# Retention outputs and their group norm with tokens on partitions, one tile at a time, ahead of the attention projection

## The reference, cut to what matters

```python
scores = jnp.einsum('bnihd,bnjhd->bnhij', qf, kf) * dmask
intra = jnp.einsum('bnhij,bnjhe->bnihe', scores, vf)
kv = jnp.einsum('bnjhd,bnjhe->nbhde', kf * k_w[:, :, None], vf)
# s_(n+1) = g_c * s_n + kv_n over the chunks of 128 tokens
inter = jnp.einsum('bnihd,nbhde->bnihe', qf * q_w[:, :, None], s_start)
o = intra + inter
mu, var = mean and variance of o over the 64 features of a head
y_ret = silu(rg) * (o - mu) * rsqrt(var + GN_EPS) * gn_w
merged = concatenate([y_ret, o_swa]) @ w_out
```

## Time and profile before

| | |
|---|---|
| Median of 3 runs | 2264.78 us (2264.5 to 2271.12) |
| The profiled execution | 2266.3 us, span 2264.4 us |
| TensorE busy | 2197.3 us of the span (97%) |
| VectorE, ScalarE, GpSimd busy | 892.3, 510.6, 520.2 us |
| Mean granted TensorE clock | 0.969 of full |
| Retention, first scores to the next block's start | 1014.98 to 1101.46 us |
| Group norm and attention projection | 1101.46 to 1216.97 us |

### The profile page before, as it was taken

The page is one execution under the profiler, slowest core; times in us unless marked ns, Lnnn a source line. Parts: engine busy times, 40 slices in busy tenths (PEclk is TensorE's granted clock), DMA queues, the critical chain, the costliest instruction groups (busy, mean ns, idle before and its releaser), DMA issues. The chain is left out here.

```text
span 2264.4 us, 31134 instructions
## 1 busy us (share of the span) xinstructions
PE 2197.3 (97%) x12045; PEld 1978.2 (87%) x12045; DVE 892.3 (39%) x1606; ACT 510.6 (23%) x877; POOL 520.2 (23%) x253
## 2 busy tenths in 40 slices
PE   8999999999999999999898889999999999999997
PEld 8999999999999889996676458799999999999996
DVE  5534434344344430012133543433443434435246
ACT  4111111111111431111123542311111111111115
POOL 4121221212212222213122522222112121221213
PEclk9999999999999999999697699999999999999999
DMA  7101011010111011110103030010101101010112
GB/s 271 56 28 56 28 56 49 34 56 28 56 42 52 29 70 66 37 32 21 65 10 140 0 114 3 29 56 28 56 28 56 46 37 56 28 56 28 56 57 79
DMA packets 37817, 118.42 MB, mean 52 GB/s; under 512 B 5879, under 2 KB 10615, under 8 KB 37503
## 3 DMA queue, kind: packets, MB, share of 16 engines
q1 hardware_dynamic: 37759, 117.61, 14.6%
HBM read 106.32 MB, written 11.27 MB: 52 GB/s over the span
## 5 line engine op out<-in xcount | busy, mean ns | idle before, releaser
L111 PE MATMUL bank<-x_hi,f_w_hi 128*128 128x362 f32 (+1 forms) x2104 | 688.3, 327 | 7.0 <-issue 5.6
L113 PE MATMUL bank<-x_hi,f_w_low 128*128 128x362 f32 (+1 forms) x2104 | 689.9, 328 | 0.0
L360 POOL TENSOR_TENSOR f_w_low<-f_w_raw,f_w_hi 128x1024 fp32r<-128x1024 f32 x132 | 317.3, 2418 | 1177.5 <-ACT f_w_hi L290 1177.5
L548 DVE TENSOR_TENSOR acc<-bank,acc 128x512 f32<-128x512 f32 x720 | 468.0, 687 | 7.0 <-PE bank L446 5.8
L111 PEld LDWEIGHTS bank<-x_hi,f_w_hi 128*128 128x128 f32 x2104 | 396.4, 188 | 9.1 <-issue 7.4
L113 PEld LDWEIGHTS bank<-x_hi,f_w_low 128*128 128x128 f32 x2104 | 395.9, 188 | 0.0
L526 DVE TENSOR_TENSOR f_h_full<-bank,f_silu 128x362 f32<-128x362 f32 (+1 forms) x132 | 70.7, 535 | 816.9 <-PE bank L113 814.6
L112 PE MATMUL bank<-x_lo,f_w_hi 128*128 128x362 f32 (+1 forms) x1056 | 345.3, 327 | 0.0
L112 PE MATMUL bank<-x_low,f_w_hi 128*128 128x362 f32 (+1 forms) x1048 | 342.9, 327 | 0.0
L444 PE MATMUL bank<-f_w_hi,f_h_hi 128*128 128x512 f32 x640 | 250.8, 392 | 0.1
L446 PE MATMUL bank<-f_w_low,f_h_hi 128*128 128x512 f32 x640 | 250.1, 391 | 0.0
(11 more groups left out here) (192 smaller groups left out, 2347.7 us busy)
## 6 DMA issues: line engine op xcount, KB each, us to landing
f_w_raw<-ffn_in SPq DMA_DIRECT2D x132, 512.0 KB, 4.4
rp_w_raw<-w_ret_in SPq DMA_DIRECT2D x16, 512.0 KB, 3.5
acc<-x_rows_in SPq DMA_DIRECT2D x2, 2048.0 KB, 11.1
kept_rows<-acc SPq DMA_DIRECT2D x8, 512.0 KB, 3.0
ow_raw<-w_out_in SPq DMA_DIRECT2D x8, 512.0 KB, 11.3
y_out<-acc SPq DMA_DIRECT2D x8, 512.0 KB, 2.6
n_rows<-ln_rows_in SPq DMA_DIRECT2D x6, 512.0 KB, 7.8
gp_stage<-w_att_in SPq DMA_DIRECT2D x6, 512.0 KB, 3.4
```

Of the source, the lines that this page charges most:

```text
L111: pe.matmul(out, wh, xh, start=first, stop=False)
L113: return pe.matmul(out, wl, xh, start=False, stop=last)
L360: pool.tensor_tensor(flat(w_lo[s][j]), flat(w_raw[s][j]), flat(w_hi[s][j]).bitcast(F32), ALU.subtract).then_inc(done, 1)
L548: dve.tensor_tensor(acc[:, t, d], down_ps[(n + 2 * s) % 4][:, :], acc[:, t, d], ALU.add).then_inc(down_free, 1)
```

## The change

In retention the outputs are computed with tokens on partitions: probabilities (128 columns wide) or decayed queries (128 wide) are now the stationary operand, and values or state stream past, 64 columns per pass. The tiles are taken in the order 0, decode, 1 to 7. The score banks are no longer doubled, so the scores of the next tile wait for both masks of the present one. The decode outputs are still computed with features on partitions, copied by ScalarE and transposed.

Group norm moves into the retention block and works on a tile of tokens: VectorE sums over features and centres, ScalarE squares and takes the root, VectorE sums and inverts, GpSimd multiplies by the inverse deviation, TensorE transposes four times, VectorE multiplies by weight and gate, ScalarE rounds, GpSimd subtracts for the low part. The decode states are done in eight halves between the tiles (256 streaming columns each). Both state stores are issued inside the block.

The second block holds the attention projection alone, with keys and values first; the transposes of the values come after the third tile, six banks rotate, and the low part of a weight tile waits for the projection that last used its buffer. The tables of the old group norm (`ones_head`, `gn_sum`, `gn_spread`) go. In the retention projection, the gate and the token-major values now lie in the region of the stored rows, so ScalarE's wait for the rows' store moves from the first evacuation to the first gate, and GpSimd waits for all rows and for the last input tile ahead of its memset and its first key copy.

```diff
+    RORDER = (0, LAST) + tuple(range(1, BLOCKS))
+    out_ps = [core.psum[:, 1024 * i:1024 * i + 1024].rearrange("p (h c) -> p h c", h=2) for i in range(2)]
+    kv_ps, dec_kv_ps = core.banks[4][:, 0:PAIRS * HD], core.banks[4][:, PAIRS * HD:2 * PAIRS * HD]
+    score_ps, turn_ps = core.banks[5:7], core.banks[7]
...
-                    mm = pe.matmul(out_ps[h][d, w * t:w * t + w], v_tok[:, n, head(t, h)],
-                                   probs[n % 2][:, h, w * t:w * t + w], start=True, stop=n == 0)
...
-                        mm = pe.matmul(out_ps[h][d, w * t:w * t + w], state[(n - 1) % 2][d, t, :],
-                                       q_dec[n % 2][d, t, 0:w], start=False, stop=True)
...
+                    out = out_ps[p % 2][:, h, HD * t:HD * t + HD]
+                    mm = pe.matmul(out, probs[p % 2][:, h, P * t:P * t + P], v_tok[:, n, head(t, h)],
+                                   start=True, stop=n == 0)
+                    if n:
+                        mm = pe.matmul(out, q_dec[p % 2][d, t, :], state[(n - 1) % 2][d, t, :], start=False, stop=True)
...
+        for p, n in enumerate(RORDER):
+            if p + 1 < END:
+                scores(p + 1)
+            if n < LAST:
+                key_values(n)
+            if p == DEC_AT + 1:
+                decode_rows(DEC_AT)
+            if n == LAST:
+                decode_output(p)
+            else:
+                output(p)
+            if p >= 2:
+                turn(p - 2)
+            if p >= 2:
+                decode_state(p - 2)
+        decode_state(2 * PAIRS - 1)
+        turn(END - 2)
+        turn(END - 1)
...
+        for p, n in enumerate(RORDER):
+            mask_scores(p)
+            if p >= 3:
+                decode_state(p - 3)
+            if n < LAST:
+                update_state(n)
+            if p:
+                centre(p - 1)
+            if p >= 3:
+                gate(p - 3)
+            if p:
+                invert(p - 1)
...
+        project(K)
+        project(V)
+        project(2)
+        pe.wait_ge(proj_free, N * (V + 1))
...
+        for n in range(3, TILES):
+            project(n)
```

More of the change, by code:

```diff
@@ L139, in gpsimd @@
     def gpsimd(pool):
-        pool.memset(ones_head[:, :], 0.0).then_inc(filled, 1)
         pool.memset(eps[:, :], EPS).then_inc(filled, 1)
         pool.memset(eps_twice[:, :], 4 * EPS).then_inc(filled, 1)
[L143 to L147, removed]
+        pool.wait_ge(filled, 2)
     def scalar(act, n):
@@ L950, in step @@
                         copy_k(t, c, 4 + 12 * t + 3 * K + c + 1)
-        pool.memset(k_tok[:, BLOCKS, :], 0.0).then_inc(zeroed, 1)
+        pool.memset(k_tok.tile(BLOCKS), 0.0).then_inc(zeroed, 1)
+        for done in (norm.kept(0), norm.kept(TOKEN_TILES - 1)):
+            pool.wait_ge(*done)
+        pool.wait_ge(norm.x_ready, TOKEN_TILES)
         pool.memset(v_tok[:, BLOCKS, :], 0.0).then_inc(zeroed, 1)
@@ new lines, in own_values @@
+        def own_values(t):
+            if t == 0:
+                pool.wait_ge(tables_in, 48)
+            else:
+                pool.wait_ge(dec_kv_done, 2 * t)
+            for h in range(2):
+                pool.tensor_tensor(
+                    v_own[:, h, :, :],
+                    v_tok[0:DEC, LAST, head(t, h)].unsqueeze(1).to_broadcast([DEC, DEC_BATCH, HD]),
+                    own[0:DEC, :].unsqueeze(2).to_broadcast([DEC, DEC_BATCH, HD]),
+                    ALU.mult).then_inc(owned, 1)
@@ L1115, in tensor @@
[L1115 to L1119, removed]
+        for p in range(END):
+            decay(p)
+            if p == 1:
+                own_values(0)
+            elif p >= 4 and p % 2 == 0:
+                own_values(p // 2 - 1)
+            if p >= 3:
+                low(p - 3)
+            if p:
+                normalise(p - 1)
+        normalise(END - 1)
+        for p in range(END - 3, END):
+            low(p)
@@ new lines, in decode_rows, with turn @@
+        def decode_rows(p):
+            pe.wait_ge(dec_read, 2)
+            for t in range(PAIRS):
+                mm = pe.transpose(out_ps[p % 2][0:DEC, 0, P * t:P * t + P], dec_out[:, t, :], ident[:, :])
+            mm.then_inc(out_done, 1)
+        def turn(p):
+            w = tokens(RORDER[p])[2]
+            pe.wait_ge(normed, p + 1)
+            if p:
+                pe.wait_ge(gated, PAIRS * p)
+            x = rows[p % 2][0:w, :, :].rearrange("p h e -> p (h e)")
+            for t in range(PAIRS):
+                mm = pe.transpose(turn_ps[:, P * t:P * t + w], x[:, P * t:P * t + P], ident[0:w, 0:w])
+            mm.then_inc(turned, 1)
@@ new lines, in decode_state @@
+        def decode_state(u):
+            t, half = u // 2, u % 2
+            pe.wait_ge(owned, 2 * t + 2)
+            pe.wait_ge(state_done, PAIRS * min(u + 2, BLOCKS))
+            if u:
+                pe.wait_ge(dec_state_done, u)
+            for h in range(2):
+                mm = pe.matmul(dec_kv_ps[HD * h:HD * h + HD, :], k_tok.tile(LAST)[0:DEC, head(t, h)],
+                               v_own[:, h, HALF * half:HALF * half + HALF, :].rearrange("p b e -> p (b e)"),
+                               start=True, stop=True)
+            mm.then_inc(dec_kv_done, 1)
@@ new lines, in invert, with gate @@
+        def invert(p):
+            w = tokens(RORDER[p])[2]
+            st = stats[p % 2]
+            dve.wait_ge(squared, p + 1)
+            dve.tensor_reduce(st[0:w, SSQ, :], squares[0:w, :, :], AX.X, ALU.add).then_inc(squares_summed, 1)
+            dve.wait_ge(deviated, p + 1)
+            dve.reciprocal(st[0:w, INV, :], st[0:w, STD, :]).then_inc(inverted, 1)
+        def gate(p):
+            a, b, w = tokens(RORDER[p])
+            dve.wait_ge(turned, p + 1)
+            if p >= 2:
+                dve.wait_ge(lo_done, p - 1)
+            for t in range(PAIRS):
+                dve.scalar_tensor_tensor(mixed[p % 2][:, t, 0:w], turn_ps[:, P * t:P * t + w], gn_w[:, t:t + 1],
+                                         gate_t[:, t, a:b], ALU.mult, ALU.mult).then_inc(gated, 1)
```

456 lines of the change are left out of this document (193 added, 263 removed).

## The result

The changed kernel takes 2298.01 us (median of 4 runs, 2296.0 to 2299.77), the kernel before 2264.64 beside it (4 runs, 2264.43 to 2271.12). The ratio is 1.0135, with a 95% interval of 1.0122 to 1.0149: slower by 33.4 us, where 22.6 were forecast. The profiled execution has a span of 2294.9 us against 2264.4, and a mean granted clock of 0.947 against 0.969. The traces so account for 30.5 us. The other 2.9 is where the profiled runs lie against the medians: 2296.74 is 1.27 under one, 2266.3 is 1.66 above the other.

The account below looks back on a forecast made before the run. TensorE, busy 97% of the span, was taken to bound the kernel. Retention +55.3 and the second block -32.7 gave +22.6 on the median 2264.8, so 2287 us; 8-in-10 range 2243 to 2299.

Parts of the forecast that it names:

- The main step: Retention: after the decode tile in second place, all seven prompt steps run at half clock, 16.0 us each.
- 64 streaming columns for 128: Retention outputs: reason given for half rate; new steps stream 64 columns, half the array time of the old ones.
- The rule that was weighed: Retention's prompt steps: a TensorE kept busy regains full rate, steps of 9.15; given only the first rival's chance.
- The first rival: Retention: prompt steps at full rate, block 96.0 us, kernel time 2242; chance 0.18.
- The second (the clock comes and goes): Retention: scores and key-values regain the rate, outputs lose it; 2274 with two full-rate steps, 2253 with five; chance 0.15.
- The pitch: Retention: one prompt output matmul at half rate takes 0.62 us, 9.9 for sixteen.
- The third rival, 0.41: Retention outputs: half-rate pitch is 0.41 since longer loads hide, 23.5 us less, time 2264; chance 0.07.
- The price of a full-rate step: Retention: a prompt step at full rate costs 9.15 us, with the output pitch left at 0.36.
- The block of retention, +58.2 against +55.3: Whole retention block: predicted to grow from 86.5 to 141.8 us, +55.3.
- the tail: End of retention: the last tile's group norm chain, 10.0 us with 2.1 already counted, so 7.9, plus block change 0.8.
- The second block, -32.4 against -32.7: Attention projection without group norm: predicted 82.8 us against 115.5, giving 32.7; bounds 28 to 36.
- The likeliest case: Whole kernel: half rate in all seven prompt steps, time 2287, own range 2275 to 2299; chance 0.60.

Follow-up runs that it names:

- e1: Changed kernel with only one of the eight sequences' state products issued in the decode tile's outputs; 2286.6 us, 1.0084 to the kernel before.
- e5: Changed kernel with the decode tile last and its updated states in a buffer of their own; 2297.1 us, 1.0114 to the kernel before.
- e12: e5 with the second tile's scores in two free banks, so TensorE has no wait ahead of the prompt steps; 2289.2 us.
- e3: Changed kernel with prompt outputs computed features on partitions as before, copied by ScalarE and turned by four transposes; 2301.5 us, 1.0149 to the kernel before.
- e4: Changed kernel with the edits of e2 and e3 together: features on partitions, full-height output matmuls before half-height ones; 2251.0 us.
- e7: e5 with the edits of e4 too: decode tile last, outputs with features on partitions and grouped by height; 2252.1 us.
- e9: e4 with VectorE's masks of the next tile right behind the state of the present one, ahead of the group norm work; 2251.7 us.
- e10: e9 with the decode tile's scores in two free banks at the start and decode outputs ordered full-height first; 2248.1 us.
- e2: Changed kernel with each tile's eight full-height output matmuls before its eight half-height ones, in place of alternating; 2274.5 us, 1.0017 to the kernel before.
- e6: e5 with the edit of e2 too: decode tile last, output matmuls grouped by height; 2271.8 us, 1.0022 to the kernel before.
- e8: Kernel before the change, with only the output matmuls of prompt tiles 1 to 7 grouped by height; 2250.5 us, 0.9915 to the kernel before.

## Why the prediction was right, and where its sizes were off

**The clock.** The main step held: the seven prompt steps run at 0.50 (e1, e5 and e12 show it with a short decode tile, with none ahead, and without a wait ahead). What I gave as the reason, 64 streaming columns for 128, is half of it. e12 shows that the new outputs lose a rate which the old ones, on the same pitch of 0.36, had kept. Up to the fall TensorE's work has the same order as in the kernel before, with no transpose of results and no state half in it yet, so the layout of the outputs is what differs. It isn't the chance of one execution either: e12's four runs took 2288.9 to 2290.0, at mean granted clocks of 0.949 to 0.951, and none of the forty runs of the kernel before that stand beside the experiments was under 0.966.

But e3 shows that the old matmuls behind the decode tile don't get the rate back either. So the changed kernel stood under two conditions, and each of them, without the other, still came with half rate from the fall to the last prompt step: the new outputs (e12) and the decode tile in second place (e3). Not run was the old layout in turn, decode tile last, with the group norm between the tiles.

What brings the rate back is not shown. It came back in e4, e7, e9 and e10, with outputs that have features on partitions and are grouped, and not in the traces of e2 and e6, grouped with tokens on partitions. Yet e4's first return stood ahead of its grouped outputs, while e9's (1051.5) and e10's (1042.7) fell among them, and e4 has four more transposes a step than e2. That both layout and grouping are needed is a conjecture. What the chip looks at isn't settled by these runs.

The rule that was weighed, of the Trainium skill, page "TensorE: Matmul & The Clock Gate", section "Why this matters for your kernels", that a TensorE kept busy gets the full rate, does not hold for busy time as the profile counts it: 102.00 of 102 us at 0.50 in e12. The first rival fell with the changed kernel's own trace. The second (the clock comes and goes) did not occur in the changed kernel, but is what e4, e7, e9 and e10 do.

**The pitch.** Forecast 0.62, measured 0.617; a full step 16.0, measured 16.03. My reasoning for it was wrong in part: I took a pitch of 0.41 with loads and passes of 64 columns, said that the load paces it, and added 0.22 for loads of 128. The growth came out (0.617 less 0.41), but in e3 the loads have 64 columns, the passes 128, and the pitch is again 0.617, so loads alone are not the reason. And the 0.41 was read across a change of height (L1151 to L1156), so the price of that change was in it unnamed; that the parts add up to the measured pitch is partly luck. What makes it is 0.35 to 0.45 of work in which one operand or the other is 128 columns wide, and 0.17 to 0.27 for each change of height (e2 at half rate; 0.36 less 0.19, so 0.17, at full rate in e8). The third rival, 0.41, is what the order of e2 comes to (0.40 on average), with the changes of height gone and not with the loads hidden. The price of a full-rate step stood too: the new output matmul at 1.00 has the 0.36 that I had left unchanged (e12).

**The block of retention, +58.2 against +55.3.** Start 8.8 (8.1), decode outputs 15.2 (16.0), from there to the last output 107.5 (106.9), behind it 13.2 (10.8). So the term that was mis-sized is the tail. VectorE's and TensorE's rows of it:

```profile
1147.41 1.11 PE L1236 MATMUL bank<-small,rt_rows 128*128 128x128 f32 x4
...
1148.63 0.69 DVE L1314 TENSOR_REDUCE rt_stats<-bank 128x8 f32<-128x512 f32 x1 [6.40 <-PE bank L1236]
...
1150.79 1.12 PE L1246 MATMUL bank<-rt_v_own,ret_k_dec 64*64 64x256 f32 x4 [1.21 <-DVE rt_state_dec L1342]
1151.94 0.48 DVE L1342 SCALAR_TENSOR_TENSOR rt_state_dec<-rt_state_dec,small,bank 128x256 f32<-128x256 f32 x1 [1.30 <-PE bank L1246]
```

Centring waits for the transposes of the tile before (its rows buffer), which stand behind the last output, 1.0; and the last state half can't start on TensorE before VectorE has read the one before, 1.3 idle on VectorE. Both waits are in the code, and I had summed durations instead of following them.

**The second block, -32.4 against -32.7.** First projection 7.2 behind the start (7.1), half rate until 1171.5 as expected, total 83.1 (82.8).

**Outside the two blocks, +4.8, which I had at nothing.** The attention stage, from its first matmul to the first of the output projection, took 125.5 us before and 129.0 after. No edit touches it. In the fourteen kernels profiled, the same in this stage, it took 125.4 to 130.3. The clock does not fall and return at the same points in all of them: three falls in the kernel before (at 1.1, 52 and 70 us of the stage), four in the changed one (at 3, 51, 68 and 85). Its 3.5 is no effect of the change that could be shown; the longer median may hold such a share too. The first scores start 0.9 later, and 0.4 lies behind.

**The chances.** The likeliest case was right in sign and in the half rate of the seven steps, its reason by half, and the time, 2298.0, lay at the upper end of its own range (2275 to 2299): tail 2.4, attention 3.5 and a start of the block 0.9 later went the same way, and 2.9 is the profiled runs against the medians. That it stayed inside the range owes something to luck, since its upper end had 5 us for start and tail and nothing for attention.

## What to carry to other kernels

Price thin float32 matmuls at both clock rates, and don't count on a busy TensorE to get the full one back: read the granted clock of the nearest rows like them, and what stood ahead of them. Put matmuls of equal operand height side by side; here that alone gave 18 us in the old kernel (2268.4 to 2250.5) and 24 in the changed one, and it cost nothing. Where work is added behind the last matmul of a block, follow its chain wait by wait.

## What the runs showed of the hardware

- Sixteen float32 matmuls that alternate between full-height and half-height operands have a pitch of 0.36 us at 1.00 and 0.617 at 0.50; in turn it made no difference which operand has 128 and which 64 columns. Grouped by height it is 0.19 at 1.00 with loads of 64 columns (e4, e8), and with loads of 128 it is 0.35 for half height and 0.45 for full height at 0.50 (e2).
- The same output matmuls ran at 1.00 for 48 us behind a projection (the kernel before) and at 0.50 for 114 us behind a decode tile that ended at 0.50, in steps with eight more transposes and a state half (e3). Behind one and the same wait of 1.23 us the rate fell in four traces and stayed in six; e12 fell without a wait.
- The attention stage varied by 4.9 us between programs in which it is the same.
